# Two unused products before the turning of the probabilities in every attention step

## The chip, the cores and the metric

The kernel runs on one core of a Trainium2 chip. The time is the device time of one execution in microseconds (us), smaller is better. Before the change three runs gave 2831.09, 2832.06 and 2833.45 us, with a median of 2832.06 us.

The engines named here: PE is TensorE (matrix products, its weight loads are shown apart as PEld), DVE is VectorE, ACT is ScalarE, POOL is GpSimd and SP is SyncE, which issues most DMAs. PSUM has eight banks here, `PS[0]` to `PS[7]`; PE writes them, DVE and ACT empty them.

## The reference

The kernel computes a stack of small transformer layers over 256 tokens of width 1024: two mixer layers with context (chunked token mixing with neighbourhood attention; Fourier mixing with gated linear attention), each with a SwiGLU FFN; one layer with latent and banded attention; one with compressed, selected and windowed attention; two cross attentions; and a mixture of eight experts at the end. What matters here is the softmax attention. In the first layer it reads, cut to its core:

```
s_nb = einsum('bqhd,bwkhd->bhqwk', qr, kb) * scale + bias
s_cx = einsum('bqhd,bchd->bhqc', qr, k_ctx) * scale
p = softmax(concatenate([s_nb, s_cx], axis=-1), axis=-1)
out = einsum('bhqk,bkhd->bqhd', p_nb, vb) + einsum('bhqc,bchd->bqhd', p_cx, v_ctx)
```

So each head has three parts: scores from queries and keys, a softmax over the keys, and a product of the probabilities with the values. All of it is in fp32.

## The kernel before, in words

There is one instruction stream for each engine, written out by hand, and semaphores between them. No scheduler reorders anything: an engine runs what stands in its stream, in that order.

All softmax attention goes through one piece of code for each engine: `attention_pe`, `attention_act` and `attention_dve`. A list of steps is handed to the three. A step holds one or two units (a unit is what fits one bank of scores, that is 128 queries by 512 scores). There are 43 steps in the program, in six lists: 12 in the first layer (called AB here), 6 of latent attention (DSA), 3 of banded attention (band), 4 in each of the two cross attentions, and 14 of the compressed and selected attention (NSA), of which the first two only make compressed probabilities.

`order(n)` gives the sequence that all three engines follow. For each a it does S of step a, then T of step a-2, then V of step a-3:

- **S**: PE multiplies queries and keys into a score bank (banks 0 to 3, line 927). DVE scales them and adds the bias into SBUF (lines 1043 and 1045; for "direct" steps it only takes the maximum from the bank, line 1038), takes the maximum of each row (line 1059) and raises `scores_ready`. ACT takes the exponential (line 965). Then DVE, still in its S of step a, divides the probabilities of step a-1 by their sums (reciprocal at line 1009, product at line 1017) and raises `probs_ready`.
- **T**: PE turns the probabilities of step a-2, four 128x128 transposes for a unit, into a "turned" bank (line 938). ACT copies the bank to SBUF (line 983) and so frees it; in the cross attentions DVE does the copy (line 1078).
- **V**: PE multiplies values and turned probabilities into an output bank, 6 or 7 (line 948), once the copies of that step are made. ACT copies the result out (line 988).

The turned banks are two, 4 and 5: unit n uses bank `4 + n % 2`. In steps with two units each step takes both, so T of step a needs the copies of T of step a-1 to be over. In steps of one unit it needs the copy of T of step a-2. ACT makes these copies in its own order: the copy of T of step a-1 stands behind the exponentials of step a+1.

`Book` counts how often each bank has been filled and emptied; `book.fill(b)` takes a bank and `book.eng.wait_ge(free(b), book.emptied())` waits until what was in it has been read.

`keep_busy` (line 456) is older code for long waits outside attention: it issues products of a 128x128 block of ones with 256 columns of the constants, in fp32, into the next bank, and nobody reads them. The change uses the same product.

A matmul of fp32 operands shows as two records in the profile; a transpose shows as one.

Of the kernel before, what the change touches and what calls it, by code (L numbers as in the profile page):

```python
# [19 lines left out]
SEQ = 256  # L20
# [87 lines left out]
def build(nc, stream, ada_stream, c_rows, small, x_t, ctx_t, mem_t, ab_bias, sgu, t5_bias, band_bias, cmp_bias, out):  # L108
    with ExitStack() as ctx:
        def sb(name, cols, dt=F32):  # L110
            return ctx.enter_context(nc.sbuf_tensor(name, [P, cols], dt))
# [3 lines left out]
        def sem(name):  # L115
            if name not in sems:
                sems[name] = ctx.enter_context(nc.semaphore(name))
            return sems[name]
# [10 lines left out]
        consts = sb("consts", N_SMALL)  # L129
# [7 lines left out]
        PS = [ctx.enter_context(nc.psum_tensor(f"bank{i}", [P, 512], F32)) for i in range(BANKS)]  # L137
# [7 lines left out]
        def small_at(name, pattern=None, **dims):  # L145
            a, w = COL[name]
            v = consts[:, a:a + w]
            return v.rearrange(pattern, **dims) if pattern else v

        ident, ones = small_at("ident"), small_at("ones")  # L150
# [161 lines left out]
        X2 = slice(0, SEQ)  # L312
# [7 lines left out]
        def full(b):  # L320
            return sem(f"bank_full{b}")

        def free(b):
            return sem(f"bank_free{b}")
# [559 lines left out]
        def order(n):  # L884
            for a in range(n + 3):
                if a < n:
                    yield "S", a
                if 0 <= a - 2 < n:
                    yield "T", a - 2
                if 0 <= a - 3 < n:  # L890
                    yield "V", a - 3

        def score_bank(n):
            return n % 4

        def turned_bank(n):
            return 4 + n % 2

        def out_bank(a):
            return 6 + a % 2  # L900
# [10 lines left out]
        def by_turns(lists):  # L911

            for m in range(max(map(len, lists))):
                for u, one in enumerate(lists):
                    if m < len(one):
                        yield u, m, one[m]

        def attention_pe(book, steps):
            turned, outs = {}, []
            for what, a in order(len(steps)):  # L920
                units = steps[a]["units"]
                if what == "S":
                    for unit in units:
                        b = book.fill(score_bank(unit["n"]))
                        book.eng.wait_ge(free(b), book.emptied())
                    for u, m, (to, q, k) in by_turns([unit["scores"] for unit in units]):
                        ins = nc.tensor.matmul(to, q, k, start=True, stop=True)
                        if m == len(units[u]["scores"]) - 1:
                            ins.then_inc(full(score_bank(units[u]["n"])), 1)
                elif what == "T":  # L930
                    book.eng.wait_ge(sem("probs_ready"), book.up("probs_ready"))
                    turned[a] = []
                    for unit in units:
                        b = book.fill(turned_bank(unit["n"]))
                        turned[a].append(book.turn - 1)
                        book.eng.wait_ge(free(b), book.emptied())
                        for j, e in enumerate(unit["turns"]):
                            ins = nc.tensor.transpose(PS[b][:, j * P:(j + 1) * P], e, ident)
                        ins.then_inc(full(b), 1)
                elif steps[a]["outs"]:  # L940
                    for taken in turned[a]:
                        book.eng.wait_ge(*book.freed(taken))
                    b = book.fill(out_bank(a))
                    outs.append(book.turn - 1)
                    book.eng.wait_ge(free(b), book.emptied())
                    values = [unit["values"] for unit in units]
                    for u, m, (to, v, p, first, last) in by_turns(values if steps[a]["halves"] else [sum(values, [])]):
                        ins = nc.tensor.matmul(to, v, p, start=first, stop=last)  # L948
                    ins.then_inc(full(b), 1)
            return outs[-2:]  # L950
# [313 lines left out]
        def _(pe):  # L1264
# [73 lines left out]
            for taken in bk.all_freed(bk.turn - 16, 12):  # L1338
                pe.wait_ge(*taken)
            attention_pe(bk, ab_steps())  # L1340
            split_products(bk, w, DC, mixed_high, h_part, TT, out_slot_high, ready="mixed_split")
            sum_pe(bk, "squared", lambda c: sq_out[:, c, :], TT)
# [183 lines left out]
            mem_products()  # L1526
            pe.wait_ge(sem("bias_landed"), 48)
            outs = attention_pe(bk, dsa_steps())
            uv = small_at("w_uv", "p (h n) -> p h n", h=8)
            for taken in outs:  # L1530
                pe.wait_ge(*bk.freed(taken))
            for h in range(8):
                b = bk.next_bank()
                pe.wait_ge(free(b), bk.emptied())
                nc.tensor.matmul(PS[b][half(h % 2), X2], uv[:, h, :], o_lat[:, h, :], start=True, stop=True)\
                    .then_inc(full(b), 1)
            outs = attention_pe(bk, band_steps())
            out_products(h_x, 1, outs)

# [1307 lines left out]
```

## Time and profile before

| | |
|---|---|
| median of three runs | 2832.06 us |
| the profiled execution | 2831.2 us, its span 2829.4 us |
| PE busy | 2670.3 us (94%) |
| DVE busy | 1937.3 us (68%) |
| ACT busy | 1160.0 us (41%) |
| chain that ended last | PE 86%, DVE 8%, ACT 3% |
| the six attention stretches together | 213 us of the span |

The span is the time from the first to the last instruction of one profiled execution; the execution's own time is 1.8 us longer. The chain that ended last follows the work back from the last instruction, at each step to what released it. Two thirds of the program are dense products in the FFNs and the experts, and there the chain is PE's. The attention stretches are the only part that the change touches: 160 to 222 us (AB), 1173 to 1197 (DSA), 1199 to 1222 (band), 1277 to 1291 and 1718 to 1733 (cross), 1589 to 1664 (NSA).

The granted clock is that of TensorE: 1.0 is 2.4 GHz, 0.5 is 1.2 GHz.

### The profile page before, as it was taken

How to read it: one execution, taken by the hardware profiler on the slowest of the kernel's cores; microseconds unless marked ns; L12 is line 12 of the kernel's file. 1: busy time of each engine (PE TensorE's matmuls, PEld its weight loads, DVE VectorE, ACT ScalarE, POOL GpSimd, SP SyncE). 2: the span in 40 equal slices, each digit the busy share in tenths (PEclk: the TensorE clock that was granted, in tenths of full speed). 3: DMA queues.
4: the chain of work that ended last, by engine and by line, in shares of the span. 5: the costliest groups of instructions: out<-in, count | busy, mean ns of one | idle time of the engine just before them, and what ended most of it. 6: DMA issues, size and time to landing. Idle time of an engine off the chain costs nothing.

```text
span 2829.4 us, 37253 instructions
## 1 busy us (share of the span) xinstructions
PE 2670.3 (94%) x14201; PEld 2224.0 (79%) x14201; DVE 1937.3 (68%) x2237; ACT 1160.0 (41%) x1452; POOL 52.6 (2%) x97
## 2 busy tenths in 40 slices
PE   7979999999989999888999888999999999999998
PEld 4857788886579998577998667888888888888886
DVE  4977766763346771636775544888787878888786
ACT  4243100002311001423001343677777777777675
POOL 0100100000000000000000000000000000000000
PEclk9989999999989999999999899999999999999999
DMA  8713544442215443122443211689898989899895
GB/s 318 282 48 134 181 169 157 170 156 106 88 45 205 181 181 121 60 84 96 179 178 134 105 60 60 261 336 350 325 375 325 374 319 372 328 348 351 316 375 212
DMA packets 90324, 598.64 MB, mean 212 GB/s; under 512 B 9728, under 2 KB 12800, under 8 KB 23552
## 3 DMA queue, kind: packets, MB, share of 16 engines
q1 hardware_dynamic: 77280, 543.20, 50.6%
q0 software_dynamic: 12960, 54.26, 5.4%
q8 instruction: 60, 0.98, 0.1%
q14 instruction: 24, 0.20, 0.0%
HBM read 596.37 MB, written 1.05 MB: 211 GB/s over the span
## 4 chain that ended last, share of the span: by engine, by line
PE 86%; DVE 8%; ACT 3%; issue 1%; DMA 1%; SPq 0%; DVEq 0%; ACTq 0%
PE bank L481 10%; PE bank L712 9%; PE bank L716 9%; PE bank L715 9%; PE bank L1678 7%; PE bank L1682 7%; PE bank L1681 7%; PE bank L1711 4%; PE bank L1714 4%; PE bank L1715 4%; PE bank L495 2%; PE bank L470 1%; PE bank L511 1%; ACT arena L965 1%; PE bank L948 1%
## 5 line engine op out<-in xcount | busy, mean ns | idle before, releaser
L608 DVE TENSOR_TENSOR ring_part<-ring,arena_part 128x2048 fp32r<-128x2048 f32 x451 | 1016.2, 2285 | 64.5 <-ACT arena_part L1957 56.5
L1957 ACT ACTIVATE arena_part<-ring 128x2048 fp32r<-128x2048 f32 x339 | 643.0, 1918 | 158.2 <-DMA ring<-in_stream 158.1
L712 PE MATMUL bank<-arena_part 128*128 128x256 f32 (+1 forms) x1744 | 571.6, 328 | 17.4 <-DVE arena_part L608 6.0
L716 PE MATMUL bank<-arena_part,ring_part 128*128 128x256 f32 (+1 forms) x1744 | 567.2, 325 | 0.0
L715 PE MATMUL bank<-h_part,arena_part 128*128 128x256 f32 (+1 forms) x1216 | 399.2, 328 | 0.0
L712 PEld LDWEIGHTS bank<-arena_part 128*128 128x128 f32 x1744 | 332.2, 191 | 55.1 <-issue 13.9
L1678 PE MATMUL bank<-arena_part 128*128 128x512 f32 x896 | 354.6, 396 | 3.3 <-issue 2.7
L716 PEld LDWEIGHTS bank<-arena_part,ring_part 128*128 128x128 f32 x1744 | 332.4, 191 | 27.1
L1682 PE MATMUL bank<-arena_part 128*128 128x512 f32 x896 | 349.7, 390 | 0.0
L1681 PE MATMUL bank<-ring_part,arena_part 128*128 128x512 f32 x896 | 348.8, 389 | 0.0
L806 ACT ACTIVATE arena<-bank 128x256 f32<-128x256 f32 (+1 forms) x66 | 29.9, 455 | 649.5 <-PE bank L716 649.4
L715 PEld LDWEIGHTS bank<-h_part,arena_part 128*128 128x128 f32 x1216 | 231.9, 191 | 19.4
L1678 PEld LDWEIGHTS bank<-arena_part 128*128 128x128 f32 x896 | 168.3, 188 | 38.3 <-issue 5.1
L1682 PEld LDWEIGHTS bank<-arena_part 128*128 128x128 f32 x896 | 168.1, 188 | 36.2
L1681 PEld LDWEIGHTS bank<-ring_part,arena_part 128*128 128x128 f32 x896 | 168.4, 188 | 33.6
L1711 PE MATMUL bank<-arena_part 128*128 128x512 f32 x448 | 176.5, 394 | 0.0
L1714 PE MATMUL bank<-ring_part,arena_part 128*128 128x512 f32 x448 | 175.8, 393 | 0.0
L1715 PE MATMUL bank<-arena_part 128*128 128x512 f32 x448 | 175.6, 392 | 0.0
L715 PE MATMUL bank<-arena_part 128*128 128x256 f32 (+1 forms) x528 | 168.2, 318 | 0.0
L481 PE MATMUL bank<-h_normed,ring 128*128 128x256 f32 (+1 forms) x672 | 153.3, 390 | 4.6 <-issue 2.3
L481 PEld LDWEIGHTS bank<-h_normed,ring 128*128 128x128 f32 x672 | 127.3, 190 | 29.7 <-issue 10.7
L2029 DVE COPY arena<-bank 128x512 f32<-128x512 f32 (+3 forms) x24 | 13.2, 556 | 179.4 <-PE bank L481 83.2
(302 smaller groups left out, 3279.7 us busy)
## 6 DMA issues: line engine op xcount, KB each, us to landing
ring<-in_stream SPq DMA_DIRECT2D x515, 1024.0 KB, 4.8
arena<-in_ada_stream POOLq DMA_DIRECT2D x80, 512.0 KB, 4.5
consts<-in_small POOLq DMA_DIRECT2D x1, 2800.0 KB, 12.9
arena<-in_c_rows POOLq DMA_DIRECT2D x2, 1024.0 KB, 7.9
arena<-in_ab_bias POOLq DMA_DIRECT2D x1, 2048.0 KB, 8.4
arena<-in_t_bias POOLq DMA_DIRECT2D x1, 2048.0 KB, 8.0
x_stream<-in_x_t SPq DMA_DIRECT2D x1, 1024.0 KB, 7.1
x_stream<-in_ctx_t SPq DMA_DIRECT2D x1, 1024.0 KB, 9.2
```

The costliest lines, as they stand in the source:

```text
L481: m = nc.tensor.matmul(PS[b][:, 0:cols], tile, rhs(k), start=k == 0, stop=k == kc - 1)
L608: return nc.vector.tensor_tensor(low, value, high.bitcast(F32), ALU.subtract)
L712: m = nc.tensor.matmul(out_ap, w_high, high, start=start, stop=False)
L715: nc.tensor.matmul(out_ap, w_high, low, start=False, stop=False)
L716: return nc.tensor.matmul(out_ap, w_low, high, start=False, stop=stop)
L1678: m = nc.tensor.matmul(PS[b][:, :], x_e_high[:, k, :], high, start=k == 0, stop=False)
L1681: nc.tensor.matmul(PS[b][:, :], x_e_high[:, k, :], low, start=False, stop=False)
L1682: m = nc.tensor.matmul(PS[b][:, :], x_e_low[:, k, :], high, start=False, stop=k == DC - 1)
L1711: m = nc.tensor.matmul(PS[b][:, :], h_high, high, start=f_blk == 0 and f == 0, stop=False)
L1714: nc.tensor.matmul(PS[b][:, :], h_high, low, start=False, stop=False)
L1715: m = nc.tensor.matmul(PS[b][:, :], h_low, high, start=False, stop=f_blk == MB - 1 and f == FB - 1)
L1957: nc.scalar.activation(high, ring[:, where], ACT.Copy).then_inc(sem("moe_high"), 1)
```

## The change

In T, PE used to wait for `probs_ready` first and then, for each unit, for its turned bank. Now it waits for the bank of the first unit, issues two products of constants into this bank (`ones` with 256 columns of `consts`), then waits for `probs_ready`, and then makes the transposes, which overwrite the bank. Nothing reads the two products. This is done in each of the 43 steps, so there are 86 products more. Nothing else in the program changes.

```diff
                 elif what == "T":
-                    book.eng.wait_ge(sem("probs_ready"), book.up("probs_ready"))
                     turned[a] = []
-                    for unit in units:
+                    for u, unit in enumerate(units):
                         b = book.fill(turned_bank(unit["n"]))
                         turned[a].append(book.turn - 1)
                         book.eng.wait_ge(free(b), book.emptied())
+                        if u == 0:
+                            for _ in range(2):
+                                nc.tensor.matmul(PS[b][:, X2], ones, consts[:, 0:SEQ], start=True, stop=True)
+                            book.eng.wait_ge(sem("probs_ready"), book.up("probs_ready"))
                         for j, e in enumerate(unit["turns"]):
                             ins = nc.tensor.transpose(PS[b][:, j * P:(j + 1) * P], e, ident)
                         ins.then_inc(full(b), 1)
```

The three lines that are added move all later lines of the file down by three: line 938 of the kernel before, the transposes, is 941 after, and 948 is 951.

On PE, in AB (two units a step), the turning of one step, from S (line 927) of the step before it to its V (line 948 before, 951 after). `bank<-consts` alone is one of the new products, `bank<-consts,arena` a transpose:

```order
 L927 MATMUL bank<-arena 128x512 [waits bank_free3,bank_free2]
 L927 MATMUL bank<-arena 128x512
-L938 MATMUL bank<-consts,arena 128x128 [waits bank_free4,probs_ready]
-L938 MATMUL bank<-consts,arena 128x128 x3
-L938 MATMUL bank<-consts,arena 128x128 [waits bank_free5]
-L938 MATMUL bank<-consts,arena 128x128 x3
+L938 MATMUL bank<-consts 128x256 [waits bank_free4]
+L938 MATMUL bank<-consts 128x256
+L941 MATMUL bank<-consts,arena 128x128 [waits probs_ready]
+L941 MATMUL bank<-consts,arena 128x128 x3
+L941 MATMUL bank<-consts,arena 128x128 [waits bank_free5]
+L941 MATMUL bank<-consts,arena 128x128 x3
```

The first transpose waited for the bank and the probabilities together. Now the two products stand between the two waits: they wait for bank 4, and only the transposes wait for the probabilities.

On PE, in DSA (one unit a step), before the change, from one T (line 938) over V (line 948) and S (line 927) to the next T:

```order
L938 MATMUL bank<-consts,arena 128x128 [waits bank_free5,probs_ready]
L938 MATMUL bank<-consts,arena 128x128 x3
L948 MATMUL bank<-arena 128x128 [waits bank_free6,bank_free4]
L948 MATMUL bank<-arena 128x128 x3
L927 MATMUL bank<-arena 128x128 [waits bank_free0]
L927 MATMUL bank<-arena 128x128 x3
L938 MATMUL bank<-consts,arena 128x128 [waits bank_free4,probs_ready]
```

Here too the two products come in front of each T, so everything behind them on PE, V and the next S, stands behind them as well.

## Rows read from the trace of the kernel before

**Rows 1.** The page: span, and busy time of each engine.
```profile
span 2829.4 us, 37253 instructions
PE 2670.3 (94%) x14201; PEld 2224.0 (79%) x14201; DVE 1937.3 (68%) x2237; ACT 1160.0 (41%) x1452; POOL 52.6 (2%) x97
```

**Rows 2.** Windows, the six attention stretches summed: length, busy time of each engine.
```profile
sum 213.00, PE 148.22 PEld 109.53 DVE 148.70 ACT 127.09 POOL 0.00; mean PE 24.70 PEld 18.25 DVE 24.78 ACT 21.18 POOL 0.00
```

**Rows 3.** Line 938, whole program: what ended PE's idle time before it (us, times).
```profile
DVE arena L1017: 52.7, 32
issue: 34.4, 19
ACT arena L983: 29.8, 22
```

**Rows 4.** Timeline, a step in NSA: start, length, engine, line, operation [idle before <-releaser].
```profile
1615.10 1.23 DVE L1017 TENSOR_TENSOR arena<-arena 128x1024 f32<-128x1024 f32 x1
1616.80 1.05 ACT L983 ACTIVATE arena<-bank 128x512 f32<-128x512 f32 x2
1617.52 1.06 PE L938 MATMUL bank<-consts,arena 128*128 128x128 f32 x8 [1.30 <-ACT arena L983]
```

**Rows 5.** Chain that ended last, behind that turning: start, length, what.
```profile
1618.58 1.24 PE bank L948 x20
1619.82 1.07 PE bank L927 x3
...
1621.01 1.30 DVE arena L1045 x2
```

**Rows 6.** Chain, turnings on it: AB, DSA, band, cross.
```profile
188.82 1.06 PE bank L938 x8
...
1193.92 0.44 PE bank L938 x4
...
1218.28 1.52 PE bank L938 x8
...
1287.96 0.44 PE bank L938 x4
```

**Rows 7.** Timeline, the first steps of AB, on PE and DVE.
```profile
175.81 1.97 PE L938 MATMUL bank<-consts,arena 128*128 128x128 f32 x8 [3.13 <-DVE arena L1017]
...
177.25 1.22 DVE L1017 TENSOR_TENSOR arena<-arena 128x1024 f32<-128x1024 f32 x1
```

**Rows 8.** Line 456, the existing products of constants (ns min/median/max).
```profile
L456 PE MATMUL bank<-consts x240: 379/379/796, 38.5 to 1783.3; 128*128 128x256 f32 x120
```

**Rows 9.** Chain, fp32 products of 256 columns without a gap.
```profile
1222.44 27.86 PE bank L481 x128
```

**Rows 10.** Windows at granted clock 0.50: one of four, and the sum of the four.
```profile
1588.00:1611.80 23.80, 18.73 (x96) 11.88 (x96) 16.39 (x35) 8.12 (x30) 0.00 (x0) 0.50 0.24 101
...
sum 57.90, PE 36.84 PEld 25.39 DVE 39.20 ACT 26.30 POOL 0.00; mean PE 9.21 PEld 6.35 DVE 9.80 ACT 6.57 POOL 0.00
```

**Rows 11.** Chain, pieces of PE at the low clock.
```profile
177.78 2.01 PE bank L927 x3
...
1608.19 1.94 PE bank L938 x8
1610.13 1.92 PE bank L927 x3
...
1656.54 2.76 PE bank L948 x24
```

**Rows 12.** Timeline, V of NSA at the full clock.
```profile
1651.69 1.53 PE L948 MATMUL bank<-arena 128*64 128x128 f32 x24
```

**Rows 13.** Timeline, a turning and the V behind it in DSA.
```profile
1185.51 0.65 PE L938 MATMUL bank<-consts,arena 128*128 128x128 f32 x4
...
1186.32 1.16 PE L948 MATMUL bank<-arena 128*128 128x128 f32 x8 [0.15 <-ACT arena L983]
```

**Rows 14.** Timeline, the second turning of band.
```profile
1214.44 1.94 PE L938 MATMUL bank<-consts,arena 128*128 128x128 f32 x8 [4.57 <-ACT arena L983]
```

## The prediction

> **What bounds the kernel now.** I read the page first. Its span is 2829.4 us, and PE is busy for 94% of it [rows 1]; outside attention the chain runs on PE with hardly a gap. The change touches only the six attention stretches. They are 213 us long together, PE is busy for 148.2 us of that and DVE for 148.7 us [rows 2], so neither fills them: here the end is set by a loop that goes from engine to engine, and an addition to PE is free or not according to where in the loop it lands. The next view is the line of the transposes, with what ended PE's idle time before them: in 32 cases the scaling on DVE (line 1017), in 19 "issue", in 22 the copy on ACT (line 983) [rows 3]. There is idle time before the turnings, about 117 us by this count over both of PE's rows, and the reader should see that it ends for two different reasons. The new products stand behind one of them, the wait for the bank, and in front of the other, the wait for the probabilities.
>
> So the question is which of the two comes last where it counts, and a step in the timeline answers it [rows 4]. The probabilities are ready at 1615.10 + 1.23 = 1616.33. The two copies on ACT, each about half of 1.05 us, begin at 1616.80. PE begins to turn at 1617.52, that is about 0.15 us after the first copy and 1.2 us after the probabilities. The bank comes last, because ACT makes this copy only behind the exponentials of a later step. PE is idle for 1.30 us before it, but the products can't use this time: they too wait for the bank. From there the chain goes on without a gap: the turning, V for 1.24 us, S for 1.07 us, and DVE fills from the score bank at 1621.01 [rows 4, 5]. A delay of the turning is a delay of the next scores, and DVE's row shows it waiting for these.
>
> **The change part by part.** *The price of two products.* The same product stands in line 456: fp32, 256 columns, two records for each product (240 records, 379 ns one by one) [rows 8]. The single record's length overlaps with its neighbour's, so the pace is what counts: 128 records of an fp32 product of 256 columns took 27.86 us without a gap, 0.218 us for each [rows 9]. Two products are four records, 4 x 0.218 = 0.87 us at the full clock, and about 1.74 us at half of it.
>
> *Where they are hidden.* In the first turning of each stretch both banks have long been free. In AB PE was idle for 3.13 us before it, until DVE's scaling at line 1017 [rows 7]; the products at half clock take 1.74 of them and cost nothing. The same holds for the first one or two turnings of DSA, band, cross and NSA. It also holds where a turning is late but its step has slack: the loop in AB and NSA hops, only one turning in three or in two stands on the chain, and the others have about a microsecond before DVE asks for their scores. I charge nothing for these at first.
>
> *Where they are not.* I count the turnings on the chain that ended last, stretch by stretch, without the first one of AB: 5 in AB (from 188.82 on), 1 in DSA (1193.92), 2 in band (the last at 1218.28), 1 in each cross attention (1287.96, and the same in the second one), and 7 in NSA (from 1608.19 on) [rows 6, 11]. The early ones of AB, band and NSA were released by ACT's copy as in [rows 4], so their bank came last. The late ones of each stretch follow the V before them at once, PE being the last to come, and there the products simply stand in line. That makes 17, and 17 x 0.87 = 14.8 us.
>
> *Slack that is used up.* In DSA a turning at 1185.51 has no idle time before it, and V at 1186.32 waits only for ACT's copy [rows 13]. With 0.87 us more the four transposes (0.44 us at their pace on the chain, rows 6) end at about 1186.8, so V and the scores behind it come 0.5 to 0.7 us late, and DVE takes them up without slack: +0.6. In AB the turnings off the chain are late too, and the direct step's maximum follows DVE's scaling closely; I take +0.5. The bounds for both together are 0 (all slack suffices) and 3 us (0.87 us once more in AB's three inner loops). I take 1.1, nearer to the lower end, since only DSA has a row that shows it.
>
> *The clock.* In four spells of attention, 57.9 us together, the granted clock is 0.50, that is 1.2 GHz [rows 10]. It fell after PE had been idle or nearly so and came back only after a stretch in which PE had worked without a gap. The new products fill gaps, so part of these spells may go. Not all of it can come back. The spells of AB and NSA begin before the first turning, and nothing is added there. What could be had, by the same pieces at the full clock: in AB the first turning 1.97 - 1.06 and S 2.01 - 1.07, together 1.85 us [rows 7, 6, 11, 5], but DVE's own scaling ends at 177.25 + 1.22 = 178.47, and S ended at 177.78 + 2.01 = 179.79, so at most 1.3 [rows 7, 11]; in NSA 1.94 - 1.06 and 1.92 - 1.07, together 1.73 [rows 11, 6, 5], and for the short spell at 1656 V 2.76 - 1.53 = 1.23 [rows 11, 12]; in band the second turning (1.94) [rows 14], the V behind it and a part of the last turning, an estimated 2.3 by the same halving. Bounds: 0 and 6.6 us. In AB and in early NSA the products fill the idle time right before the first transposes, and in late NSA they stand in the gap after which the clock fell: I take 1.3, 1.7 and 1.2, together 4.2. In band the turned bank is freed so late that PE is idle for 4.57 us before the second turning [rows 14] and the products can't go there, so I take 0. A product that runs in a spell costs 1.74 instead of 0.87, but as long as the spell ends at the same time it keeps 0.87 us of other work out of the slow time, so I count 0.87.
>
> The Trainium skill has a rule on this ("TensorE: Matmul & The Clock Gate", Part 4: PE-mode transpose): a transpose doesn't count as a busy PE in the way that a product does. If it holds, the kernel before had less activity in attention than its busy time says, and the products would weigh more. The trace neither shows nor excludes it: the clock came back at 1611.8 us behind 3.9 us of transposes and score products mixed [rows 10, 11]. By the rule the clock term would go toward its upper bound, 6.6, and the sum to 9.3; by the rows alone it stays at 4.2.
>
> **The sum.** 14.8 + 1.1 - 4.2 = +11.7 us. Nothing behind an attention stretch takes this up: the products after each stretch need its output, and the weight ring has long been full. The profiled execution took 2831.2 us, so it would take 2842.9; the median of the runs lies 0.9 above it. I predict 2843 us, between the two.
>
> **The rivals.** *A: the clock gives nothing back.* The spells end and begin as before. For it: in the spell of NSA PE was busy for 18.73 of 23.80 us and the clock stayed at half until its end [rows 10]. Against it: the gap before those transposes is just what is filled now. 2831.2 + 14.8 + 1.1 = 2847; should band's spell last longer because everything moves, 2849.
>
> *B: the clock gives all of it back.* All that is said under the clock, band too: 2831.2 + 15.9 - 6.6 = 2840.5. Even then the kernel is slower, since at the full clock everywhere the 17 turnings still cost 14.8 us. The Trainium skill's advice to keep TensorE from idling between bursts (same page, Part 1: The HAM clock gate) would favour B.
>
> *C: not slower.* The products run in the idle time before the turnings after all. Its place is the wait for the turned bank: a releaser is inferred, and had ACT's copy freed the bank in truth 0.9 us or more before the probabilities came, the products would end before the transposes could begin. The point from which it decides is that difference; at 1617 us the trace has it the other way round by 1.2 us, and the order on ACT (copy behind exponentials) says the same. With it the cost is 0 to 2 us and the clock gives 4 to 6.6: 2825 to 2829. Only the 32 idle spans that ended with DVE speak for it; they are mostly at the beginning of stretches or where the first bank was free but the slack is not on the chain.
>
> *D: the products cost less than their pace,* since the turning that follows starts its first weight load under them: at most the pace of one transpose, 1.06 / 8 = 0.13 us [rows 4], for each of 17, or 2.2 us, which gives 2841. It lies within the forecast.
>
> **How the numbers follow.** The forecast, with its own range of 2840.5 to 2845.5 (the clock 2 to 6, the slack 0.5 to 1.5), gets 0.58. A gets 0.20, B 0.14, C 0.04, and 0.04 goes to a mixture in which half of the 17 are hidden, at about 2836. The range of 2838 to 2848.5 leaves out C, the mixture and the far end of A. What a measurement of this kernel can tell from no change is about 0.2%, 5.7 us: slower means above 2837.7. Slower gets 0.91 (forecast, A and B, less a little of B's lower end), within 0.2% 0.06 (the mixture, part of C and of B), faster 0.03.
>
> **What would show it.** In the profile after, the products before a turning released by ACT should begin where the turning began before, about 0.15 us after the first copy, and the turning should follow 0.87 us later with no idle time and no wait for `probs_ready`. From one turning on NSA's chain to the next should be 0.87 us longer. AB should be about 4 us longer, NSA 3 to 4, band 1 to 2, each cross attention 0.9, DSA about 1.5. The short spell at half clock near 1656 should be gone, and those of AB and NSA end earlier. I would be wrong if the products lay in PE's idle time and the turnings began when they did before, or if the stretches outside attention changed.

## The result and the profile after

The changed kernel took 2844.7 us as the median of five runs (2843.97 to 2848.66), against 2832.06 us before. The medians are 12.6 us apart. The ratio is 1.0048, with a 95% interval of 1.0037 to 1.0060: 10.5 to 17 us slower. The forecast was 2843 us.

The profiled execution of the changed kernel was the slowest of its five, 2848.66 us, so the two traces lie further apart than the medians. The page, the lines that answer to [rows 1]:

```profile
span 2846.9 us, 37554 instructions
PE 2706.4 (95%) x14373; PEld 2257.4 (79%) x14373; DVE 1937.2 (68%) x2237; ACT 1160.9 (41%) x1452; POOL 52.6 (2%) x97
```

PE has 172 records more, two for each of 86 products; DVE and ACT do what they did. Next, the two lines in the view by source, what ended PE's idle time before them (us, times; both of PE's rows are counted, matrix products and weight loads). The products, line 938:

```profile
L938 PE MATMUL bank<-consts x172: 379/379/794, 172.7 to 1748.3; 128*128 128x256 f32 x172
...
ACT arena L986: 55.4, 33
issue: 3.9, 8
```

And the transposes behind them, line 941:

```profile
DVE arena L1020: 19.2, 12
issue: 0.6, 3
```

Line 986 is the copy of the turned bank (983 before), 1020 the scaling that makes the probabilities (1017 before). Compare with [rows 3]: DVE ended 32 spells of PE's idle time there, 12 here, and 19.2 us of it. The wait in which the products were to hide ended with ACT's copy in 33 spells, before the products began.

The timeline of two steps in NSA (start, length, engine, line, operation, tiles [idle before <-releaser]) answers to [rows 4, 5]:

```profile
1623.34 1.23 DVE L1020 TENSOR_TENSOR arena<-arena 128x1024 f32<-128x1024 f32 x1
...
1625.04 1.05 ACT L986 ACTIVATE arena<-bank 128x512 f32<-128x512 f32 x2
1625.66 1.13 PE L938 MATMUL bank<-consts 128*128 128x256 f32 x4 [1.22 <-ACT arena L986]
...
1626.63 1.04 PE L941 MATMUL bank<-consts,arena 128*128 128x128 f32 x8
...
1629.90 1.13 PE L938 MATMUL bank<-consts 128*128 128x256 f32 x4
1630.10 1.29 DVE L1048 SCALAR_TENSOR_TENSOR arena<-bank,arena 128x512 f32<-128x512 f32 x2 [1.37 <-PE bank L927]
```

The probabilities were ready at 1624.57. PE was idle for 1.22 us until the first copy had been made, then ran the four records, and the transposes began 0.97 us after the products, without idle time. DVE then waited 1.37 us for the scores behind them; in the same place before (1621.01 in [rows 5]) it had waited 0.52 us.

The chain that ended last has the products in it at each such step (start, length, what):

```profile
1625.13 0.49 ACT arena L986
1625.66 1.13 PE bank L938 x4
1626.79 0.87 PE bank L941 x8
1627.67 1.24 PE bank L951 x20
1628.91 1.07 PE bank L927 x3
...
1635.35 1.13 PE bank L938 x4
```

From one turning on the chain to the next it is 9.69 us; before the change 8.83 us (1617.52 in [rows 4] to the next one at 1626.35).

To see where the time went I measured each attention stretch in the trace, from the start of its first score product to the start of its last value product, with the time at half clock inside it:

| stretch | before | after | change | forecast, by its terms | half clock before, after |
|---|---|---|---|---|---|
| AB | 60.86 | 65.18 | +4.32 | +3.6 | 17.1, 6.8 |
| DSA | 22.31 | 23.42 | +1.11 | +1.5 | 0, 0 |
| band | 21.70 | 23.17 | +1.47 | +1.7 | 13.7, 10.2 |
| first cross | 12.91 | 13.78 | +0.87 | +0.87 | 0, 0 |
| NSA | 73.43 | 78.69 | +5.26 | +3.2 | 25.7, 19.0 |
| second cross | 12.90 | 13.78 | +0.88 | +0.87 | 0, 0 |
| sum | 204.11 | 218.02 | +13.91 | +11.7 | 56.5, 36.0 |

Outside these stretches the profiled execution was 3.6 us longer than that of before. The prediction had named a change there as a sign of being wrong. In this execution 72.8 us of the rest ran at half clock, against 62.1 before. A second profile of the same program was 2.4 us shorter there than before, with 59.1 us at half clock (below), so the 3.6 us are no effect of the change that can be told from chance.

### The profile page after: what moved, and what is told of

Its sections match the earlier page's. It is cut to its first block, busy times and chain, and to the rows that moved or that the text cites. A ratio compares the mean times of both kernels' runs of the same rounds, so it can differ in the third digit from the quotient of the medians.

```text
span 2846.9 us, 37554 instructions
## 1 busy us (share of the span) xinstructions
PE 2706.4 (95%) x14373; PEld 2257.4 (79%) x14373; DVE 1937.2 (68%) x2237; ACT 1160.9 (41%) x1452; POOL 52.6 (2%) x97
## 4 chain that ended last, share of the span: by engine, by line
PE 87%; DVE 8%; ACT 3%; issue 1%; DMA 1%; SPq 0%; DVEq 0%; ACTq 0%
PE bank L481 10%; PE bank L712 9%; PE bank L716 9%; PE bank L715 9%; PE bank L1681 7%; PE bank L1685 7%; PE bank L1684 7%; PE bank L1714 4%; PE bank L1718 4%; PE bank L1717 4%; PE bank L495 2%; PE bank L470 1%; PE bank L951 1%; PE bank L511 1%; ACT arena L968 1%
```

## The experiments

In each, "longer" or "shorter" is the sum of the six stretches in the profile, against 204.11 us before. The ratio is that of the timed runs, with its interval.

**The dose.** One product, and four, in place of two:

```diff
-                            for _ in range(2):
+                            for _ in range(1):        # one_product
+                            for _ in range(4):        # four_products
```

> One product instead of two in each of the 43 turnings, all else as in the changed kernel. Theory (the turned bank is the last to come, so a product stands on the chain in the 17 turnings that are on it): 17 x 0.436 = 7.4 us, less 1 to 3 us that the clock gives back, so +4 to +7 us against before. Rival 1 (not the products but the swap of the two waits, or the new wait between products and transposes, costs the time): +12 us as with two. Rival 2 (the first product is hidden in some rest of a wait and only the second is not): 0 to +2 us.

> Four products instead of two. Theory: 17 x 1.74 = 29.7 us on the chain, and turnings off the chain now use up their slack too, less 1 to 4 us of clock: +27 to +34 us. Rival 1 (the swap of the waits costs the time): about +12 us. If the clock were what decides, four would hold it up in all attention spells and the gain of 6.6 us would show: +24 us.

One product: 2838.78 us, ratio 1.0027 (1.0017 to 1.0038), stretches 6.8 us longer. Four: 2868.85 us, ratio 1.0128 (1.0113 to 1.0144), 32.4 us longer. With two it was 13.9. So the products cost the time, each of them from the first on, and both rivals fall: the swap alone would have cost the same with one, two and four, and a hidden first product would have left +2 us at most. The two cross attentions, which have no spell at half clock, give the price without anything else in it: +0.43, +0.87 and +2.90 us for one, two and four. The first two are the 0.436 us of one product once and twice. Four products, 1.74 us, cost 1.16 more than that. In that trace the chain passes the products of all four turnings of a cross attention, and PE has no gap from the first scores to the last value product: the slack is used up, and PE alone sets the length.

By the timed runs the four products cost more than was expected, about 36 us where +27 to +34 was written. In the profile 7.4 us of this lie outside the stretches, with 81.0 us at half clock there; no run tells whether they are chance.

**Which turnings.** Two products, not in the last two turnings of each list, and then only in these:

```diff
-                            for _ in range(2):
+                            for _ in range(2 if a < len(steps) - 2 else 0):    # not_last_two
+                            for _ in range(0 if a < len(steps) - 2 else 2):    # last_two_only
```

> Two products in the same place, but not in the last two turnings of each list of steps. Theory: of the 17 turnings on the chain 3 in AB and 5 in NSA are left, 8 x 0.87 = 7.0 us, with 1 us of used slack, less 2 to 4 us of clock: +4 to +6 us. Rival (the cost is the same for each of the 43 turnings, 12.6 / 43 = 0.29 us): 31 turnings are left, +9 us.

> Two products in the turned bank only in the last two turnings of each list. Theory: on the chain 2 in AB, 1 in DSA, 2 in band, 1 in each cross attention and 2 in NSA, 9 x 0.87 = 7.8 us, with hardly any clock given back: +7 to +8 us in the attention stretches, and with the kernel without the last two (6.2) it adds up to the 13.9 of the full change. Rival (0.32 us for each of the 43): 12 turnings, +3.9 us.

Without the last two: 2838.75 us, ratio 1.0026 (1.0016 to 1.0036), 6.2 us longer; AB +2.56, DSA +0.24, NSA +3.36, and band and cross by 0.03 us at most. Only the last two: 2839.79 us, ratio 1.0030 (1.0020 to 1.0040), 7.6 us longer; AB +1.81, DSA +0.88, band +1.34, cross +0.87 and +0.88, NSA +1.78. The two halves add up: 6.2 + 7.6 = 13.8 against 13.9. The last two turnings of each list, 12 of the 43, cost more than half of it, where an even cost would have given them 3.9 us. With only these, each stretch but band, which has a spell at half clock, is longer by nearly a whole multiple of 0.87. By the timed runs alone, the first half lies between the two expectations (+7.4 us, where 4 to 6 and 9 were written).

**The waits alone.** No products, the two waits in the new sequence:

```diff
-                            for _ in range(2):
-                                nc.tensor.matmul(PS[b][:, X2], ones, consts[:, 0:SEQ], start=True, stop=True)
```

> No product at all, only the two waits in the new sequence (the bank first, then the probabilities). Theory: the first transpose waits for both either way, so 0 +/- 1 us in the attention stretches. Rival (the order of the waits costs something in each turning): 1 us or more.

2831.27 us, ratio 1.0000 (0.9991 to 1.0009), 0.2 us shorter. AB is 0.01 us from its length of before although its time at half clock was 13.7 instead of 17.1: a part of such a spell falls where PE has nothing to do (before the change it was idle for 7.60 us up to 170.60, most of that inside the spell that begins at 164.6). The swap costs nothing.

**Another bank, first try.** If the wait for the turned bank is what exposes the products, another bank should hide them. The output bank of the step, before both waits:

```diff
+                    if a < len(steps) - 2:
+                        o = out_bank(a)
+                        book.eng.wait_ge(free(o), book.filled_in[o])
+                        for _ in range(2):
+                            nc.tensor.matmul(PS[o][:, X2], ones, consts[:, 0:SEQ], start=True, stop=True)
```

> The same two products in the same turnings as in the kernel without the last two, but written into the output bank of the step, which is free long before the turned bank, and issued before both waits. Theory: the products now lie in PE's idle time (0.8 to 1.7 us before the turnings on the chain), cost nearly nothing, and the clock gives back 2 to 4 us: -4 to 0 us against before. Rival (products in front of a turning cost their time wherever they are written, since PE has no real idle time there): +4 to +6 us as in the other kernel.

2841.78 us, ratio 1.0036 (1.0022 to 1.0050), 10.2 us longer, against 6.2 with the same products in the turned bank. Both expectations were too low: the products cost more here than in the turned bank. The timeline of AB shows why:

```profile
194.67 1.09 ACT L989 ACTIVATE arena<-bank 128x512 f32<-128x512 f32 x2
...
195.62 0.41 ACT L994 ACTIVATE h_normed<-bank 128x256 f32<-128x256 f32 x1
...
196.09 1.13 PE L935 MATMUL bank<-consts 128*128 128x256 f32 x4 [0.83 <-ACT h_normed L994]
...
197.06 1.04 PE L944 MATMUL bank<-consts,arena 128*128 128x128 f32 x8
```

Line 989 copies the turned banks and 994 the output. ACT does the output behind the copies, so the output bank comes free last of all: the products began at 196.09, 0.8 to 0.9 us after the first copy had freed the turned bank. I had looked at when PE had filled the output bank and not at where its emptying stands in ACT's stream.

**Another bank, second try.** The score bank of the following step. DVE (or ACT, in a direct step) has emptied it before the copies that the turning waits for:

```diff
-                        o = out_bank(a)
+                        o = score_bank(steps[a + 1]["units"][0]["n"])
```

> The output bank was the wrong place: ACT copies the output behind the turned banks, so it comes free 0.7 us later than they do. Here the same two products (not in the last two turnings) go into the score bank of the following step, which DVE has emptied before the exponentials that the copies wait for. Theory (what costs time is that the products wait for a bank that comes last): they now lie in PE's idle time of 0.8 to 1.7 us before the turnings on the chain; the attention stretches together, 6.2 us longer in the kernel with the products in the turned bank, become 0 to 1 us longer by the products and 1 to 3 us shorter by the clock: -3 to +1 us. Rival (products between S and the turning cost 0.87 us in a turning on the chain wherever their wait ends): 6 us longer, as with the turned bank.

2828.01 us against 2831.01 of before beside it, ratio 0.9989 (0.9980 to 0.9997), and the stretches 0.9 us shorter: the same products in the same turnings, and the cost of 6.2 us is gone. The timeline of NSA in this kernel:

```profile
1645.14 1.13 PE L927 MATMUL bank<-arena 64*128 64x256 f32 x8
1646.20 1.13 PE L935 MATMUL bank<-consts 128*128 128x256 f32 x4
...
1646.44 1.05 ACT L989 ACTIVATE arena<-bank 128x512 f32<-128x512 f32 x2
1647.17 1.04 PE L944 MATMUL bank<-consts,arena 128*128 128x128 f32 x8
...
1650.44 1.13 PE L935 MATMUL bank<-consts 128*128 128x256 f32 x4
...
1652.27 1.06 ACT L989 ACTIVATE arena<-bank 128x512 f32<-128x512 f32 x2
1652.90 1.14 PE L944 MATMUL bank<-consts,arena 128*128 128x128 f32 x8 [1.33 <-ACT arena L989]
```

The products follow the scores at once, before or while ACT copies. At 1652.90 PE is still idle for 1.33 us behind them and turns when the copy is done, as it did before the change. NSA became 2.01 us shorter: it had 13.0 us at half clock instead of 25.7, and none from 1616 to 1664. In the cross attentions, where less than 0.87 us is idle, it cost 0.41 and 0.42 us, in DSA 0.25, in AB 0.14.

**Only where it paid.**

```diff
-                    if a < len(steps) - 2:
+                    if len(steps) == 14 and a < 12:                             # score_bank_nsa_only
+                    if len(steps) in (12, 14) and a < len(steps) - 2:           # score_bank_ab_nsa
```

> Two products in the score bank of the following step, in NSA's first 12 turnings alone. With them in all six stretches NSA became 2.0 us shorter, the cross attentions 0.4 us longer each, DSA 0.25 and AB 0.14 longer. Theory: the gain is the clock in NSA and the losses are the turnings with less than 0.87 us of idle time; alone it gives NSA -2.0 and nothing elsewhere, -2 us (2829). Rival (NSA's gain was where its spells happened to fall, not the products): NSA within 1 us of before, no change of time.

> The same in AB and NSA, each without the last two turnings. Theory: AB +0.1 (its turnings have 0.8 to 1.7 us of idle time, and the clock comes back a little earlier), NSA -2.0, the others unchanged: -2 us. Rival as for NSA alone.

In NSA alone: ratio 0.9995 (0.9986 to 1.0004), NSA 2.41 us shorter, all other stretches within 0.13 us. In AB and NSA: ratio 0.9997 (0.9988 to 1.0006), NSA again 2.41 us shorter, AB 0.19 shorter, but DSA 0.90 longer with a spell of 6.8 us at half clock, where before it had none. So the gain in NSA came in three of three profiles (2.0 to 2.4 us), where the two profiles without any product (before, and the waits alone) differ by 0.10 us. It is hardly chance, but in the two narrower kernels it is less than the timed runs can tell from nothing. Against expectation the times of the two narrower kernels aren't lower than that of the wide one; their intervals overlap with its own.

**Products or transposes.** Seven transposes of the block of ones for the two products, in the turned bank:

```diff
-                            for _ in range(2):
-                                nc.tensor.matmul(PS[b][:, X2], ones, consts[:, 0:SEQ], start=True, stop=True)
+                            for _ in range(7):
+                                nc.tensor.transpose(PS[b][:, 0:P], ones, ident)
```

> In place of the two products seven transposes of the block of ones into the turned bank, in all 43 turnings: 7 x 0.133 = 0.93 us of PE for each, about the length of the two products (0.87). Theory: the cost is PE's time behind the bank, whatever the instruction is, so the attention stretches become 17 x 0.93 = 15.8 us longer, less what the clock gives back (about 1 to 2 us with the products): +13 to +16 us. If transposes don't hold up the clock as products do, the time at half clock in attention stays near the 56.5 us of before, where the two products brought it to 36.0, and the sum is at the upper end or above it.

2844.66 us, ratio 1.0047 (1.0034 to 1.0060), the stretches 10.5 us longer, less than the +13 that was expected at least. The length of seven was mis-sized: in the timeline of the cross attention they take from 1290.80 to 1291.57, 0.77 us, that is 0.110 us each and not 0.133.

```profile
1290.80 0.93 PE L938 MATMUL bank<-consts 128*128 128x128 f32 x7
1291.57 0.60 PE L941 MATMUL bank<-consts,arena 128*128 128x128 f32 x4
```

The cross attentions became 0.77 and 0.78 us longer, exactly that. So the cost is PE's time behind the bank, whatever runs in it. On the clock it is open: 46.1 us at half clock in the stretches, against 36.0 and 42.8 in two profiles with products and 56.5 before; NSA had 15.4 us, less than with products (19.0), and DSA a spell of 3.4 that it doesn't have with them. One profile doesn't separate this.

**The change once more**, for a second profile.

> The changed kernel once more, for a second profile: how far do the attention stretches and the spells at half clock differ between two executions of the same program? Theory (the cost is 0.87 us in each turning on the chain): cross and DSA as before to 0.1 us (0.87 and 1.1 us longer than before the change), AB, band and NSA within 1 to 2 us of the first profile, because their spells at half clock fall elsewhere; 13 to 15 us in all, and +12 to +14 us in time. Rival (the first profile was an odd one and half of its 13.9 us came from spells): 10 us or less.

2844.95 us, ratio 1.0047 (1.0033 to 1.0061). The stretches were 14.0 us longer: +4.59, +1.12, +1.36, +0.87, +5.21, +0.88. The first profile was no odd one: no stretch differs by more than 0.3 us between the two, even AB, which had 6.8 us at half clock in one and 13.7 in the other. Outside the stretches this execution was 6.0 us shorter than the first, with 59.1 us at half clock against 72.8. So the two spans, 2841.0 and 2846.9 us, differ outside the code that was edited.

## Why the prediction was right, and which term was off

**The bank comes last: right.** What the prediction wanted to see of it is in the trace: products right after the first copy (it ends at 1625.13 + 0.49 = 1625.62 on the chain, they begin at 1625.66), transposes behind them with no idle time, 9.69 us a loop. The experiments show it from the other side: with the products in a bank that is free earlier their cost is gone, in one that is free later it is larger.

**The price, 0.87 us: right** in the cross attentions and DSA's last two turnings (0.87 and 0.88). Where PE was released by a copy, it is 0.97 us from the first product to the first transpose, but the products begin 0.04 us after the copy where the transposes had begun 0.14 us after it (1617.52 in [rows 4], with the copy's end at 1617.38 on the chain), so 0.87 again is what is added. Rival D, a cheaper product, falls.

**The count of 17: right as a cost, not as a count.** The chain of after crosses the products 20 times. In AB it does so 7 times, not 5:

```profile
179.74 1.13 PE bank L938 x4
...
188.78 1.13 PE bank L938 x4
...
197.83 1.13 PE bank L938 x4
...
201.92 1.06 PE bank L938 x4
...
210.89 1.13 PE bank L938 x4
...
219.11 1.13 PE bank L938 x4
...
222.14 1.06 PE bank L938 x4
```

DSA has 2 and not 1, NSA 7, band 2 and each cross attention 1, as counted. A turning that comes onto the chain costs only what is left over from its slack, and not 0.87. The forecast put this under the used slack, with +0.5 in AB and +0.6 in DSA. In DSA it was about 0.24 (all but the last two turnings cost that much by themselves). In AB it was about 0.87, at the second turning, which had been charged nothing; this follows from the next part. Together that is the 1.1 of the forecast, but from the wrong places.

**The clock, -4.2 us: the mis-sized term.** Attention became 13.9 and 14.0 us longer where the sum gave 11.7. If the products are taken at 14.8 and the used slack at 1.1, the clock gave back about 2.0 us and not 4.2. This split is a reckoning and no measurement; only the sum of each stretch is measured. By stretches it is 0.9 in AB (1.3 in the forecast), 0.3 in band (0) and 0.8 in NSA (2.9): 7 x 0.87 = 6.1 in NSA, and it became 5.3 longer.

In AB the clock did come back earlier, at 174.6 instead of 181.6, and the first turning and its scores ran fast, 1.09 and 1.13 us for the 1.97 and 2.01 of [rows 7, 11]:

```profile
175.88 1.09 PE L941 MATMUL bank<-consts,arena 128*128 128x128 f32 x8 [1.15 <-DVE arena L1020]
176.91 1.13 PE L927 MATMUL bank<-arena 64*128 64x512 f32 x4
179.74 1.13 PE L938 MATMUL bank<-consts 128*128 128x256 f32 x4 [1.70 <-ACT arena L986]
```

But the next turning could not begin before ACT's copy. PE stood idle for 1.70 us and began the products at 179.74; before the change the second turning had begun at 179.75 with no idle time. The V behind it began at 181.67, before the change at 181.62, in a stretch that begins 0.07 us later: no net gain. What the clock gave back, about 0.9 us, was just used up by the second turning's products. From there to its end AB fell 4.3 us behind in this profile and 4.6 in the second, where 5 x 0.87 is 4.35.

In NSA the first spell ended early, as predicted. The turning that took 1.94 us before [rows 11] took 1.04 at 1622.35. Two of the seven turnings later, at the V of 1631.83 (1618.51 before), NSA was only 0.06 us behind, so on this path the clock had given back about 1.7, the value of the forecast. But the late spell did not go away. The windows at half clock in NSA (start and end, length, busy time of PE, PEld, DVE, ACT, POOL, then the clock):

```profile
1601.30:1615.00 13.70, 12.20 (x78) 9.93 (x80) 7.22 (x20) 1.20 (x3) 0.00 (x0) 0.50 0.42 173
...
1656.00:1659.40 3.40, 3.40 (x12) 2.89 (x12) 1.97 (x4) 3.40 (x17) 0.00 (x0) 0.50 0.00 0
1669.60:1673.00 3.40, 3.40 (x25) 3.07 (x25) 1.65 (x4) 3.40 (x16) 0.00 (x0) 0.50 0.00 0
```

There are two late spells where there was one, both fall on the chain, and the second profile of the same program has the same two, 1650.2 to 1653.6 and 1663.9 to 1667.3 us. The products themselves ran slow in the first:

```profile
1655.98 2.07 PE L938 MATMUL bank<-consts 128*128 128x256 f32 x4 [2.39 <-ACT arena L986]
1657.85 1.79 PE L941 MATMUL bank<-consts,arena 128*128 128x128 f32 x8
```

What this cost is seen in the V of every second step, before the change (two lines) and after it (two lines):

```profile
1636.19 1.31 PE L948 MATMUL bank<-arena 128*64 128x128 f32 x20
1646.28 1.31 PE L948 MATMUL bank<-arena 128*64 128x128 f32 x20
```
```profile
1651.22 1.31 PE L951 MATMUL bank<-arena 128*64 128x128 f32 x20
1663.81 1.31 PE L951 MATMUL bank<-arena 128*64 128x128 f32 x20
```

It was 10.09 us from one to the next and became 12.59, 2.50 more, where the steps before had added 0.86 at a time. So the loop with the first late spell in it cost 1.6 us more than its products.

The products could not stand in the 2.39 us of idle time before them, since it ends with the bank. That goes against the prediction's own second paragraph: it says there that the products can't use such idle time, sees it again for band, and for late NSA takes 1.2 us all the same, for a gap that the products never reached. That step failed, and it is 2 us of the forecast: 1.2 that did not come, and about 0.8 that the late spells cost on top.

Whether the idle time brought the late spells is supported and not proved. With the products in the score bank no late spell was seen, in three profiles of three. But that PE has something to do ahead of the gap isn't needed for it: with the products in the output bank, and with four in the turned bank, they stand behind the gap and there was no late spell either, in one profile of each:

```profile
1665.09 1.13 PE L935 MATMUL bank<-consts 128*128 128x256 f32 x4 [1.71 <-ACT h_normed L994]
```
```profile
1684.73 1.99 PE L938 MATMUL bank<-consts 128*128 128x256 f32 x8 [1.52 <-ACT arena L986]
```

What goes with the spells is how long PE was idle at a time in late NSA. Its longest idle time from 30 us behind the start of NSA on was 1.5 to 1.7 us in the five profiles without a late spell and 2.1 to 2.8 us in the eight with one or two. It doesn't tell where a spell falls: with one product it stood behind 1.82 us of idle time and none behind 2.82. The prediction's sentence that the clock fell after PE had been idle or nearly so is too strong as well: before NSA's first spell, from 1584 to 1588, PE was busy for 2.60 of 4 us.

Band gained a little (+1.47 and +1.36 for 1.74). The Trainium skill's rule that transposes do not count as a busy PE ("TensorE: Matmul & The Clock Gate", Part 4) would have put the sum at 9.3; the clock term went the other way. No run here shows or excludes the rule: the one with seven transposes doesn't decide on it.

**The rivals.** A (nothing from the clock, +15.9 in attention) came as near as the forecast: 13.9 us lies halfway between 11.7 and 15.9. By time, both medians, 2844.7 and 2844.95 us, lie nearer to the forecast's 2843 than to A's 2847, but by 0.1 to 0.6 us only, and that they do is luck: the five runs of the changed kernel are spread over 4.7 us, and the range held A too. So the time speaks for the bank and the price, and not for the clock term. B, all of the clock's 6.6 us back, fell with the 2.0. C, not slower, fell by the place of the wait, and its mechanism is what the score bank kernel makes true.

## What to carry to other kernels

A gap before an instruction is free room only for work that doesn't wait for what ends the gap. Before something is put "into the wait", find which of the waits ends last where the chain passes, and find it in the stream of the engine that raises it: here two banks that PE had finished with long ago came free late, because their copies stood behind exponentials or behind other copies. And a faster clock in a loop over three engines is worth only the part by which PE, and not its release, sets the next step.

## What had not been expected of the hardware

- Seven transposes of the same block follow each other at 0.110 us, eight of different blocks at 0.133 us (1.06 us, [rows 4]).
- Spells at half clock move by several us between executions of one program and cost a stretch next to nothing in some places: AB had 6.8 and 13.7 us of it in two profiles of the changed kernel, which differ by 0.27 us in length, and 17.1 and 13.7 without products, 0.01 us apart.
- Outside attention the time at half clock varied from 58.3 to 81.0 us between profiles without any edit there; two profiles of one program differ by 6 us of span by this. It bounds what one profile can tell of a whole kernel, while single stretches repeat to some tenths of a microsecond.
